# Prompt attention of a hybrid decoder layer: how a unit of projections is cut into pieces between the steps of attention

## The reference, cut to what matters

```python
h = rms_norm(x, g_norm)
(q, k_cmp, v_cmp, k_slc, v_slc, k_win, v_win, gate, z_a,
 q_g, k_g, v_g, log_a, z_b, merge) = mixer_inputs(h, w_in, a_up, a_b)
...
def attend(q, k, v, bias, mask):            # per branch, per block of 128 queries
    s = einsum(q, k) * scale + bias         # scores
    p = masked_softmax(s, mask)             # exp(s - max), 0 where masked
    return einsum(p, v), p                  # values
...
o_nsa = gate[0] * o_cmp + gate[1] * o_slc + gate[2] * o_win
```

## Time and profile before

| | |
|---|---|
| median of three runs | 1743.23 us (1736.05 to 1755.82) |
| the profiled execution | 1749.01 us, its span 1746.9 us |
| TensorE (PE) busy over the span | 1461.2 us, 84% |
| ScalarE (ACT) busy | 634.7 us, 36% |
| VectorE (DVE) busy | 604.1 us, 35% |
| steps of attention with units | from about 470 to 1083 us of the span |
| PE busy in 480 to 1086 us | 600.90 of 606.00 us |
| ACT busy in 480 to 1086 us | 354.77 of 606.00 us |

### The profile page before, as it was taken

One profiled execution on the slowest core, in us unless ns is written; L12 is line 12 of the kernel. 1 busy time (PEld: TensorE's weight loads), 2 busy tenths in 40 slices (PEclk: granted clock), 3 DMA queues, 4 the chain that ended last, 5 costly groups with the idle time before them and its releaser, 6 DMA issues. The chain is left out here.

```text
span 1746.9 us, 23012 instructions
## 1 busy us (share of the span) xinstructions
PE 1461.2 (84%) x9273; PEld 1267.4 (73%) x9273; DVE 604.1 (35%) x1268; ACT 634.7 (36%) x1080; POOL 109.3 (6%) x153
## 2 busy tenths in 40 slices
PE   3999939978799999999999998455686628899698
PEld 3999939967688888888888887243365518899585
DVE  4200122226233344433333332324533544343322
ACT  4111214222234576557557654104433311111211
POOL 1100011022000000000000000220000030000000
PEclk9899969998899999999999999696777758899799
DMA  8211153211122111211121111522220154422421
GB/s 237 85 42 49 58 132 93 74 45 34 45 54 65 53 51 54 66 50 58 55 61 54 54 42 32 187 100 74 101 101 4 52 178 124 153 75 62 145 97 42
DMA packets 140361, 137.03 MB, mean 78 GB/s; under 512 B 26848, under 2 KB 125360, under 8 KB 140064
## 3 DMA queue, kind: packets, MB, share of 16 engines
q1 hardware_dynamic: 137440, 127.10, 23.8%
q0 software_dynamic: 2816, 8.46, 1.7%
HBM read 97.82 MB, written 41.88 MB: 80 GB/s over the span
## 5 line engine op out<-in xcount | busy, mean ns | idle before, releaser
L215 PE MATMUL ps<-hH,wH 128*128 128x352 f32 (+1 forms) x1320 | 457.3, 346 | 7.8 <-DVE hL L471 5.7
L215 PE MATMUL ps<-hH,wL 128*128 128x352 f32 (+1 forms) x1320 | 429.7, 325 | 0.0
L215 PE MATMUL ps<-hL,wH 128*128 128x352 f32 (+1 forms) x1320 | 429.3, 325 | 0.0
L215 PEld LDWEIGHTS ps<-hH,wH 128*128 128x128 f32 (+1 forms) x1320 | 252.2, 191 | 59.9 <-issue 41.2
L215 PEld LDWEIGHTS ps<-hL,wH 128*128 128x128 f32 (+1 forms) x1320 | 252.5, 191 | 3.4 <-issue 2.5
L215 PEld LDWEIGHTS ps<-hH,wL 128*128 128x128 f32 (+1 forms) x1320 | 250.9, 190 | 0.9
L202 DVE TENSOR_TENSOR wL<-w_raw,wH 128x1024 fp32r<-128x1024 f32 (+1 forms) x55 | 66.7, 1214 | 217.8 <-ACT wH L194 212.2
L317 ACT ACTIVATE stg<-ps 128x352 f32<-128x352 f32 x132 | 61.2, 464 | 178.3 <-PE ps L215 177.6
L1158 ACT ACTIVATE pPT<-ps 128x512 f32<-128x512 f32 (+3 forms) x104 | 48.6, 468 | 129.2 <-PE ps L952 114.5
L1107 DVE CUSTOM_DVE_ANT_0 sP<-ps,dist 128x128 f32<-128x128 f32 (+3 forms) x128 | 57.6, 487 | 106.6 <-PE ps L952 70.0
L194 ACT ACTIVATE wH<-w_raw 128x1024 fp32r<-128x1024 f32 (+1 forms) x55 | 57.3, 1042 | 101.7 <-issue 101.0
(11 more groups left out here) (309 smaller groups left out, 2123.7 us busy)
## 6 DMA issues: line engine op xcount, KB each, us to landing
w_raw<-in_w_in SPq DMA_DIRECT2D x46, 512.0 KB, 4.0
p_spill<-stg SPq DMA_DIRECT2D x132, 176.0 KB, 1.8
zt<-p_spill SPq DMA_DIRECT2D x24, 528.0 KB, 3.7
gvT<-p_spill SPq DMA_DIRECT2D x8, 528.0 KB, 4.7
rq<-p_spill SPq DMA_DIRECT2D x8, 528.0 KB, 6.5
x_all<-in_x_prompt SPq DMA_DIRECT2D x8, 512.0 KB, 6.7
w_raw<-in_w_in SPq DMA_DIRECT2D x16, 256.0 KB, 6.5
S<-in_state_gla SPq DMA_DIRECT2D x4, 1024.0 KB, 5.4
```

The lines of the kernel that those rows point to most:

```text
L215: mm = nc.tensor.matmul(ps[0:t.m, bank, 0:NF], w[:, c % 2, t.m * k:t.m * k + t.m], x[:, k, NF * n:NF * n + NF], start=(k == 0 and i == 0), ...
```

## The change

`pe_half` becomes `pe_third`. A unit's 8 blocks are cut 3, 3 and 2 (9, 9 and 6 matmuls) in place of 4 and 4 (12 and 12). The first third stays between the scores and the transposes, the second goes between the transposes and the values, the third behind the values, ahead of `spread` where there is one, and of the next step's scores. The signal `u_done` goes with the last third, so it now comes after the values of its step.

```diff
-        def pe_half(pe, half):
+        def pe_third(pe, third):
...
-            if half == 0:
+            if third == 0:
                 if n == 0:
                     pe.wait_ge(sem("w_low"), c + 1)
                 if u >= 2:
                     unit_out(pe, u - 2)
-            mm = ring.products(c, n, bank, hH, hL, 4 * half, 4 * half + 4)
-            if half == 1:
+            mm = ring.products(c, n, bank, hH, hL, (0, 3, 6)[third], (3, 6, 8)[third])
+            if third == 2:
                 mm.then_inc(sem("u_done"), 1)
                 unit["pe"] += 1
...
                     if m + LA < ncut:
                         scores(*ahead[m + LA])
-                    pe_half(pe, 0)
+                    pe_third(pe, 0)
                     transposes(n, m, c, w)
+                    pe_third(pe, 1)
                     if m >= 1:
-                        pe_half(pe, 1)
                         values(*ahead[m - 1])
-                    else:
-                        pe_half(pe, 1)
+                    pe_third(pe, 2)
                     if c == 0 and closes(n - 1):
                         spread((n - 1) // 4)
```

## The result

| | before | changed |
|---|---|---|
| runs | 1743.23, 1736.05, 1755.82, 1752.23 | 1801.89, 1803.47, 1805.50, 1809.76 |
| median | 1747.73 us | 1804.49 us |
| ratio | | 1.0334, 95% interval 1.0265 to 1.0403 |
| profiled execution, span | 1749.01, 1746.9 us | 1801.89, 1799.8 us |

The change makes the kernel 3.3% slower. The forecast was 1795 us, range 1781 to 1817. From one profiled execution to the other it is +52.9 us; the forecast said +52.

A forecast was written before the change was run, and what follows sets the result against it. TensorE's own pace plus small waits for ScalarE's exponentials bounds the attention steps. Longer waits (32.7 us) and more switches (19.7) give +52 us; against the median of 1743.2 that makes 1795 us, range 1781 to 1817.

The forecast's parts named there:

- The edge: Transposes' wait for ScalarE's exponentials in attention steps, already at its limit: 22 waits, 9.9 us in all.
- part 1: Later u_done takes values and three products out of TensorE's cover, so transposes wait longer for exponentials: +32.7 us.
- chain: ScalarE's write-out, table load and two exponentials, from a unit's last product to the second exponential: 3.87 us, unchanged.
- cover: TensorE work queued between a unit's last product and the transposes; after the change 1.80 us plus the scores.
- Part 2: A third group of products per attention step adds matmul switches on TensorE: +19.7 us, ends 11.5 and 19.7.
- The rule against the trace: The skill's 1.38 us drain beside each table load, some 40 us more over 29 chains; the forecast followed the trace.
- The clock's rival: Eleven new TensorE waits of 1.6 us or more each let the clock fall, costing 19 us more: 1814; chance 12%.
- a sign of being wrong: Granted clock leaving 1.00 in the attention stretch, listed among the signs that would show the forecast wrong.
- The chain was what shrank: Answers a rival written "The chain is not what shrinks": only the added switches cost time, 1763 us; chance 8%.
- Switches did not get cheaper: Answers a rival: products behind values switch cheaper, 8 us less; with the waits gone too, 1727 us; chance 3%.
- What costs nothing: Same matmuls, banks and weights, VectorE's scoring, spread's wait, transposes' copies, later stages and DMA were to add no time.

The follow-up runs named there:

- halves_late_signal: Kernel before, no matmul moved, but u_done given by the last but one value matmul behind the unit; ratio to before 1.013, attention stretch 626.1 us.
- pieces_4_3_1: The change with a unit cut into 4, 3 and 1 blocks (12, 9, 3 products); ratio to before 1.022, attention stretch 646.9 us.
- thirds_early_exp: The change with ScalarE's exponentials moved ahead of the unit's write-out; ratio to before 1.008, attention stretch 620.7 us.

## Why the prediction was right

**The edge and part 1** held as sized. Forecast: waits from 8.3 to 41.0 us, +32.7. Measured from start to start: 8.5 to 41.2, +32.7. Nor did errors cancel: the eight rows of the second head pair, forecast at 0.67, 1.39, 1.83, 1.18, 1.10, 1.92, 1.31 and 1.60 us, measure 0.68, 1.38, 1.84, 1.16, 1.11, 1.91, 1.33 and 1.60. Only the very last row is longer, 2.2 us (1.52 and 0.70) for a forecast of 2.0. The reason is that next to nothing in this sum was a guess: chain and cover were both timed in the trace before, the change moved only a border between them, and the wait was already above zero in some rows, so no slack of unknown size lay between. halves_late_signal shows the mechanism by itself, pieces_4_3_1 its slope, thirds_early_exp its removal.

**Part 2** was forecast at +19.7 us, and the switches measure +19.7. The one price without a row, product to scores, was taken from its upper bound, 0.25 us, and is 0.25. Missed were 2.9 us of small things: the clock behind the last row's wait (1.5), spreads, which behind products run 0.05 us slower (0.8 in all), and 0.6 us of rest, chiefly from transposes to products.

**The rule against the trace.** The drain that the Trainium skill (ScalarE: Activation LUTs, What ACT_TABLE_LOAD costs) puts beside each load does not show: the chain is 3.52 us in step 22 after as it was 3.51 before, and in both the exponential starts 0.01 to 0.02 us behind the load. Taking the sigmoids out left 4.9 us of waits by starts, where a chain shorter by 1.30 us was to leave 6; had it become shorter by 2.66 us, none would be left, since the longest wait is 2.2 us.

**The rivals.** The clock's rival had its mechanism happen once, not eleven times: behind the longest wait, at a price of 1.5 us and not 19. The other waits, up to 1.9 us in two pieces, left the clock at 1.00, and 1814 is out. The prediction had named a clock under 1.00 as a sign of being wrong; it came, but too small to decide anything. The chain was what shrank. Switches did not get cheaper: values to products stayed at 0.20 us in every step. What costs nothing did cost nothing: from scores to a unit's first product, where banks and weights are waited for, all starts sum to 36.1 us in both kernels.

**The rest, and what was luck.** The 9.5 us between the forecast and the median of 1804.49 are 2.9 us in the stretch, and the median before, which lies at 1747.73 with a fourth run, 4.5 us over the one that the forecast started from. The remaining 2.1 us lie within the runs' spread. That the profiled executions differ by 52.9 us, so near to +52, is in part luck: the stretch grew by 2.9 us more than forecast, and the code around it, which is the same, happened to take 2.4 us less. One bound of the forecast is off by its own sum, 1795 less 8 and 7 being 1780 and not 1781; nothing hangs on it.

## What to carry to other kernels

When work is cut finer to cover gaps, first ask what signal its last piece carries, and who stands in line behind that signal: here one edit in ScalarE's order was worth 42 us of the stretch, and the finer cut was a loss even without the wait. Each change of matmul shape has a price that a trace shows between starts; a piece must hide more than two of them. A wait that is already visible, though it is small, is the place to compute first, since everything taken from its cover comes out one for one. And the mean of a clock over hundreds of us does not show a fall of a few: ask for it right behind the longest waits.

## What the runs showed of the hardware

- A change of the part of the array that matmuls use (128x64, 64x128 or all of it) made the next start later by about the same, whatever came. From the last value matmul to scores or to a product it was 0.20 us, where values to a spread, which use the same part, take 0.10. From the last transpose to values it was 0.20, where transposes follow each other at 0.11. From a product to values, scores or a spread it was 0.25, where products follow each other at 0.16. The second product behind scores or values then came 0.27 behind the first in place of 0.16. Transposes and products both use the whole array; between them it is 0.03, with the second product 0.24 on, which together is the pace without a change (0.11 and 0.16). By the Trainium skill (TensorEngine Tiling (Array Packing), Key Properties) a change of tiling mode drains the engine; these starts, 0.09 to 0.10 us later each, fit it.
- New waits of up to 1.9 us, in two pieces with one or a few transposes between them (at most 1.30 us in one), left the granted clock at 1.00. The wait of step 94, 1.52 and 0.70 us, was followed by 3.4 us at half of the clock, with products 0.29 us apart in place of 0.16; so was one wait of 1.73 us in a later stage. In the two kernels with the late write-out 4 of 26 undivided waits of 1.6 to 2.3 us were. So the length of a wait alone does not tell.
- The code behind the stretch, the same in all kernels but for the order of the last write-outs and the sigmoids left out, took 658 to 675 us in thirteen profiled executions. A gain of 9 us inside the stretch can hide in that.
